# Attention output written transposed by its own products, and state space output products in four column tiles

## What is computed

```python
# memory attention (4 heads of 128, 256 keys) and latent attention (8 heads, values of 64)
s = jnp.einsum('bqhd,bkhd->bhqk', q, k) * scale        # the latent one with a mask over chunks of 64
pr = jax.nn.softmax(s, axis=-1)
o = jnp.einsum('bhqk,bkhd->bqhd', pr, v)               # then o @ w_o (1024 columns)

# state space branch: 32 groups of 64 complex states, 16 channels each
y = (jnp.einsum('blgp,gcp->blgc', h_re, c_re)
     - jnp.einsum('blgp,gcp->blgc', h_im, c_im))
y = y.reshape(b_, l_, SSM_WIDTH) + d * u
z = jax.nn.gelu(y)                                     # then z @ w_glu

merged = gates[0] * br_a + gates[1] * br_b + gates[2] * br_c
x = x + merged @ w_out
x = x + hierarchical_moe(rmsnorm(x, g_ffn))            # 32 experts, two per token
```

## Time and profile before

| | |
|---|---|
| median of 3 runs | 646.52 us (645.71 to 647.54) |
| profiled execution | 645.93 us |
| its span, first to last instruction | 644.1 us |
| granted TensorE clock, mean | 0.999 |
| TensorE busy (MATMUL rows) | 611.7 us, 95% |
| weight loads | 378.5 us, 59% |
| VectorE busy | 329.3 us, 51% |
| ScalarE busy | 170.9 us, 27% |
| GpSimd busy | 149.7 us, 23% |
| HBM | 149.9 MB read and written, 233 GB/s over the span |

### The profile page before, as it was taken

The page is one execution under the profiler, slowest core; times in us unless marked ns, Lnnn a source line. Parts: engine busy times, 40 slices in busy tenths (PEclk is TensorE's granted clock), DMA queues, the critical chain, the costliest instruction groups (busy, mean ns, idle before and its releaser), DMA issues.

```text
span 644.1 us, 9883 instructions
## 1 busy us (share of the span) xinstructions
PE 611.7 (95%) x3674; PEld 378.5 (59%) x3674; DVE 329.3 (51%) x878; ACT 170.9 (27%) x540; POOL 149.7 (23%) x341
## 2 busy tenths in 40 slices
PE   9999999999999999999999999998999999986785
PEld 6788867776556667666677767853443343332341
DVE  2434846868874588783133322675435335334233
ACT  5534234321678433221100101121221121120100
POOL 1695726733584433410000000000000000000000
PEclk9999999999999999999999999999999999999999
DMA  9783553222301523323389991098999999999993
GB/s 301 176 284 115 193 159 99 66 67 93 101 2 33 168 95 99 99 66 98 107 236 404 399 386 64 10 383 345 417 417 413 418 416 417 417 418 417 416 409 126
DMA packets 61681, 150.55 MB, mean 234 GB/s; under 512 B 12352, under 2 KB 40448, under 8 KB 53696
## 3 DMA queue, kind: packets, MB, share of 16 engines
q1 hardware_dynamic: 61632, 149.89, 62.7%
HBM read 147.12 MB, written 2.76 MB: 233 GB/s over the span
## 4 chain that ended last, share of the span: by engine, by line
PE 83%; SPq 9%; DVE 4%; DMA 2%; ACT 1%; issue 1%
PE PS L819 30%; PE PS L829 20%; SPq L704 6%; PE PS L1188 5%; PE PS L1096 5%; PE PS L1227 3%; SPq L708 3%; PE PS L1217 3%; DMA E<-in_w_e 2%; PE PS L943 2%; PE PS L966 2%; PE PS L894 2%; PE PS L883 1%; PE PS L800 1%; PE PS L1008 1%; PE PS L951 1%
## 5 line engine op out<-in xcount | busy, mean ns | idle before, releaser
L819 PE MATMUL PS<-hT,W 128*128 128x320 f32 x448 | 125.9, 436 | 0.0
L819 PEld LDWEIGHTS PS<-hT,W 128*128 128x128 f32 x448 | 83.6, 190 | 37.5 <-issue 5.2
L1188 PE MATMUL PS<-E,xT 128*32 128x256 f32 x1024 | 58.6, 379 | 9.5 <-issue 8.4
L1188 PEld LDWEIGHTS PS<-E,xT 128*32 128x32 f32 x1024 | 35.4, 110 | 36.9 <-issue 20.4
L2152 POOL TENSOR_SCALAR means<-sums 128x4 f32<-128x4 f32 (+3 forms) x35 | 7.9, 225 | 189.2 <-ACT junk L1325 188.2
L1096 PE MATMUL PS<-h,S 128*128 128x512 f32 (+1 forms) x96 | 48.2, 625 | 0.7 <-DVE S L1939 0.7
L1227 PE MATMUL PS<-yb,WG 128*128 128x512 f32 (+1 forms) x96 | 40.9, 622 | 4.0 <-DVE X L2080 3.1
L829 PE MATMUL PS<-W,hT 128*128 128x256 f32 (+5 forms) x256 | 41.7, 353 | 0.0
L2080 DVE TENSOR_TENSOR X<-X,PS 128x512 f32<-128x512 f32 (+1 forms) x48 | 32.9, 686 | 8.3 <-PE PS L1227 6.7
L829 PEld LDWEIGHTS PS<-W,hT 128*128 128x128 f32 (+1 forms) x256 | 31.5, 163 | 8.4 <-issue 1.3
L829 PE MATMUL PS<-W,mergedT 128*128 128x384 f32 (+3 forms) x192 | 35.7, 381 | 0.0
(11 more groups left out here) (313 smaller groups left out, 959.0 us busy)
## 6 DMA issues: line engine op xcount, KB each, us to landing
E<-in_w_e SPq DMA_DIRECT2D x93, 1024.0 KB, 21.8
W<-in_w_in SPq DMA_DIRECT2D x7, 1536.0 KB, 7.2
W<-in_w_in SPq DMA_DIRECT2D x7, 1024.0 KB, 6.6
W<-in_w_mem_kv SPq DMA_DIRECT2D x4, 1024.0 KB, 6.1
W<-in_w_glu SPq DMA_DIRECT2D x4, 768.0 KB, 8.0
W<-in_w_out SPq DMA_DIRECT2D x2, 1536.0 KB, 15.4
E<-in_w_e SPq DMA_DIRECT2D x6, 512.0 KB, 18.8
X<-in_x_prompt SPq DMA_DIRECT2D x4, 512.0 KB, 4.4
```

Source lines behind the costliest of these rows:

```text
L819: ins = mm(out[:, 0:TOK], w[:, k, cols:cols + 128], rhs[:, k, :], start=(k == 0), stop=(k == kt - 1))
L1188: ins = mm(PS[r:r + B, 2 + par, 0:FF], xT[:, k, place_ + B * n:place_ + B * n + B], E13[slot][:, :, k, 128 * j:128 * j + 128], start=(k == ...
```

## The change

- The step OT is gone. O makes the output feature-major at once: the values are stationary (128 columns for memory, 64 for latent), PT streams (128 or 64 columns); with values of 64, two heads go to the two column halves of the array (`across_ = 2`). ScalarE empties O straight into `oTmem` or `oTmla`.
- The division by the sums moves from the output to P: `shares(m)` on VectorE waits until the exponentials are there, takes the reciprocal and multiplies the whole of P(m) in place. It runs at VectorE's step S(m+1), ahead of that step's maximum; for the last unit at its own step PT. TensorE's PT(m) waits for it (`shares_ready`).
- `s5_y(t)` makes the products of four turns at once in four column tiles, at turns 5, 9 and 13 and at the end. There are five state buffers (`STATES`) in place of four.
- The order list changes with it: without OT, `spent` grows less, and some turns start at another step. Turn 6 came before gateC(3) and now comes behind it, directly ahead of memory's PT(4). SyncE's load of the first expert waits for the last O in place of the last OT.

```diff
+STATES = 5
@@ attention_order
-            if n - 1 == len(units) or units[n - 1][1] != units[n - 2][1]:
-                yield "OT", units[n - 2][1]
@@ emptier
-        return {"S": "act", "PT": "act", "O": "dve", "OT": "act"}[unit[1]]
+        return "act"
@@ block.tensor
-            def s5_y(q):
-
-                t = q // 4
-                pe.wait_ge(s["h_state"], q + 2)
-                if q % 4 == 0 and t > 0:
+            def s5_y(t):
+
+                pe.wait_ge(s["h_state"], 4 * t + 4)
+                if t > 0:
                     pe.wait_ge(s["y_skipped"], t)
                 for c in range(2):
-                    for n in (q, q + 1):
-                        r = 32 * (n % 4)
-                        ins = mm(PS[r:r + 32, YB, 0:TOK], wC[:, c, t, r:r + 32], hS[:, n % 4, c, :], start=(c == 0), stop=(c == 1))
+                    for n in range(4):
+                        r = 32 * n
+                        ins = mm(PS[r:r + 32, YB, 0:TOK], wC[:, c, t, r:r + 32], hS[:, (4 * t + n) % STATES, c, :], start=(c == 0), stop=(c == 1))
@@ s5_turn
-                if q % 2 == 1 and q > 1:
-                    s5_y(q - 3)
+                if q % 4 == 1 and q > 1:
+                    s5_y(q // 4 - 1)
@@ attention
                     elif step == "PT":
-                        emptied((kind, "S", m))
+                        pe.wait_ge(s["shares_ready"], unit0 + m + 1)
...
-                        dv = MD if mem_ else VH
-                        for x in range(nh):
+                        across_ = 1 if mem_ else 2
+                        for i in range(heads // across_):
                             for b, rows_ in enumerate(kb):
-                                for c in range(parts):
-                                    h = h0 + nh * c + x
+                                for r in range(across_):
+                                    c, x = divmod(across_ * i + r, nh)
+                                    h = h0 + across_ * i + r
...
-                                    ins = mm(out[n * c:n * c + n, dv * x:dv * x + dv], PT[0:rows_, m % 2, at:at + n], rhs,
+                                    w = 128 // across_
+                                    ins = mm(out[w * r:w * r + w, n * i:n * i + n], values, PT[0:rows_, m % 2, at:at + n],
@@ block.vector
+                def shares(m):
+                    _, nh = across(units[m])
+                    nk = sum(key_blocks(units[m]))
+                    w = soft[:, (unit0 + m) % 4]
+                    dve.wait_ge(*emptied_at(UNIT_NO[kind, "S", m]))
+                    link(V_.reciprocal(w[:, 2, 0:nh], w[:, 1, 0:nh]))
+                    p = P[:, m % 2, 0:nh * nk].rearrange("p (h k) -> p h k", h=nh)
+                    V_.tensor_tensor(p, p, w[:, 2, 0:nh, None].broadcast_to([128, nh, nk]), ALU.mult).then_inc(s["shares_ready"], 1)
+
+                if step == "PT" and m == len(units) - 1:
+                    shares(m)
                 if step == "S":
+                    if m > 0:
+                        shares(m - 1)
```

More of the change, by code:

```diff
@@ L225, in attention @@
     def attention(kind, units, each):
-        whole = []
         for step, m in attention_order(units):
-            if step == "OT":
-                whole.append(m)
-                continue
             if m == len(units) - 1 and step in ("PT", "O"):
@@ L235, in attention @@
                 fill(each)
-                while whole:
-                    put(kind, "OT", whole.pop(0))
-        return whole
     started = False
@@ L263, in middle @@
             fill()
-    whole = attention("mem", MEM_UNITS, 1)
+    attention("mem", MEM_UNITS, 1)
     for t in range(NT):
@@ L271, in middle @@
         put("qlT", t)
-    for t in whole:
-        put("mem", "OT", t)
     for j in range(len(KEYS)):
@@ L288, in middle @@
     held, pace, due = False, LATE_PACE, spent
-    whole = attention("mla", MLA_UNITS, 1)
+    attention("mla", MLA_UNITS, 1)
     fill(1)
-    for t in whole:
-        put("mla", "OT", t)
     while turn < GP:
@@ L486, in build @@
         (ckT, qlT, V, kT), _ = place(at8, ("ckT", [128, 2, 576]), ("qlT", [128, 3, TOK]), ("V", [128, 5, 512]), ("kT", [128, H, 576]))
-        (braw, bpad, craw, cpad), _ = place(at9, ("braw", [128, 2, GP, CH]), ("bpad", [128, 2, GP, 2, CH]), ("craw", [128, 2, 4, ST]),
+        (braw, bpad, craw, cpad), at10 = place(at9, ("braw", [128, 2, GP, CH]), ("bpad", [128, 2, GP, 2, CH]), ("craw", [128, 2, 4, ST]),
                                             ("cpad", [128, 2, 4, 2, ST]))
-        (P, PT, O), at10 = place(at9, ("P", [128, 2, 512]), ("PT", [128, 2, 512]), ("O", [128, NT, 512]))
+        (P, PT), _ = place(at9, ("P", [128, 2, 512]), ("PT", [128, 2, 512]))
         (early,), at11 = place(at10, ("early", [128, NEARLY]))
@@ L719, in _ @@
             sp.dma_start(brow[:, NG:], a["b_re"][0].rearrange("g e -> (g e)").partition_broadcast(128)).then_inc(s["router_loaded"], 16)
-            done(("mla", "OT", NT - 1))
+            done(("mla", "O", len(MLA_UNITS) - 1))
             load_up(0)
@@ L921, in attention @@
                     out = begin((kind, step, m))
[L922 to L929, removed]
+                    unit0 = 0 if mem_ else len(MEM_UNITS)
+                    _, t, h0, heads = units[m]
                     f, n = TILES[t]
@@ L1019, in branch @@
                     if d == 0:
-                        emptied(("mem" if kind == "outC" else "mla", "OT", NT - 1))
+                        emptied(("mem", "O", len(MEM_UNITS) - 1) if kind == "outC" else ("mla", "O", len(MLA_UNITS) - 1))
                     feature_major((kind, d), use(f"{kind}{g}"), col, oTmem if kind == "outC" else oTmla, 4)
@@ L1042, in _ @@
                 elif kind == "last_y":
-                    s5_y(GP - 2)
+                    s5_y(GP // 4 - 1)
             pe.wait_ge(s["z_ready"], 4)
@@ L1406, in attention @@
                 unit0, oT = (0, oTmem) if kind == "mem" else (len(MEM_UNITS), oTmla)
-                if step == "OT":
-                    f, n = TILES[m]
-                    empty(oT[:, :, f:f + n], full((kind, "OT", m))[:, 0:4 * n].rearrange("p (j n) -> p j n", j=4))
+                t, n = units[m][1], 128
+                if step == "O":
+                    f, n = TILES[t]
+                    j0, nj = (x * (MD if kind == "mem" else VH) // 128 for x in units[m][2:])
+                    empty(oT[:, j0:j0 + nj, f:f + n], full((kind, "O", m))[:, 0:nj * n].rearrange("p (j n) -> p j n", j=nj))
                     return
-                t, n = units[m][1], 128
                 _, nh = across(units[m])
@@ L1701, in turn_back @@
                 cos_, sin_ = tabs[q % 2][:, 0, :], tabs[q % 2][:, 1, :]
-                if q >= 4:
-                    dve.wait_ge(s["y_full"], q - 3)
+                if q >= STATES:
+                    dve.wait_ge(s["y_full"], q - STATES + 1)
                 st.after(scanned[q])
-                dst = hS[:, q % 4]
+                dst = hS[:, q % STATES]
                 m1 = st.mark(V_.tensor_tensor(dst[:, 0], rotB[:, 0], cos_, ALU.mult))
@@ L1726, in attention @@
             def attention(kind, units, step, m):
-                if step not in ("S", "O"):
-                    return
                 unit0 = 0 if kind == "mem" else len(MEM_UNITS)
[L1730 to L1734, removed]
-                if step == "S":
+                def shares(m):
[8 more added lines that the diff above has]
+                    shares(m)
+                if step == "S":
+                    if m > 0:
+                        shares(m - 1)
+                    t, n = units[m][1], 128
+                    _, nh = across(units[m])
+                    nk = sum(key_blocks(units[m]))
+                    w = soft[:, (unit0 + m) % 4]
                     src = full((kind, "S", m))[:, 0:nh * nk]
@@ L1745, in attention @@
                             .then_inc(s["scores_max"], 1)
[L1746 to L1755, removed]
             def turned(out, x, cos_, sin_, a_, b_):
```

8 lines of the change are left out of this document (4 added, 4 removed).

## The result

The changed kernel takes 648.79 us (median of 11 runs, 647.81 to 651.21), against 646.52 (645.57 to 647.54, 11 runs) before: ratio 1.0041, 95% interval 1.0029 to 1.0052. It is slower by 2.3 us. The forecast was 646.1, no measurable difference; 648.79 lies in its range of 641.0 to 650.4, close to the 649.4 of rival E (the clock falls in the longest pause), which had a chance of 0.07.

What follows compares the result with a forecast made beforehand. TensorE was taken to set the pace up to 418 us, with the DMA-bound expert stage passing changes through; work of -8.45 and waits of 8.0 gave -0.45, so 646.52 became 646.1 us, range 641.0 to 650.4.

Steps and rivals of the forecast that it cites:

- rival E: TensorE's clock falls in the 3.55 us pause ahead of memory's PT(4): 647.8 to 650.4, say 649.4; chance 0.07.
- s5_y: State space output products: four calls of 1.20 us in place of eight, four column tiles running at once; 4.80 us less.
- OT: Transposes of the attention output: six steps vanish from TensorE's chain; 2.68 us less.
- O, latent prompt tiles: Latent attention's output products, six units at 0.60 us each in two column tiles; 1.63 us less.
- O, memory sample tile: Memory attention's output products for the sample tile: 16 loads of 128 columns, 1.68 against 1.02; 0.66 us more.
- work alone: Sum of TensorE's work changes in state space output, output transposes and output products, without new waits: -8.45 us.
- wait of PT(0) and PT(1): Memory attention's first two transposes of P wait for VectorE to scale the shares; 2.2 us together.
- wait of PT(4): Memory's last transposes of P wait while VectorE does turn 6's six operations, then the shares; 3.55 us.
- wait of latent PT(3): Latent attention's transposes of P wait for shares because VectorE is behind from turn 11 to turn 12; 1.8 us.
- wait of gateB(5): Projection in latent attention needs the bank that S(4)'s later exponentials empty; 0.4 us.
- Rivals A and B: New attention waits: A, none real, 638.1, chance 0.09; B, only the 3.55 us one, 641.6, chance 0.18.
- C: VectorE's shares stretch to 1.28 us beside GpSimd's table building, 3.6 us more in the attention waits: 649.7; chance 0.13.

Runs made afterwards that it cites:

- run 3: Changed kernel with the state space output products in pairs of turns, two column tiles and four state buffers as before; 652.74 us, ratio 1.0090.
- run 4: Changed kernel with the scaling of all shares from the second unit on one step sooner in VectorE's queue; 640.86 us, ratio 0.9910.
- run 5: Changed kernel with turn 6 put back before gateC(3), as in the kernel before; 643.14 us, ratio 0.9944.
- run 2: Changed kernel with seven unread products on TensorE filling the wait ahead of memory's PT(4); 646.54 us, ratio 1.0001.
- run 1: Changed kernel with the shares of memory's last unit scaled one step sooner on VectorE, ahead of turn 6; 643.11 us, ratio 0.9947.

## Why the prediction failed

Compared with before, in us:

| term | predicted | measured, and where |
|---|---|---|
| s5_y | -4.80 | -4.7: 8 x 1.20 less 4 x 1.22; 4.6 by run 3 |
| OT | -2.68 | gone |
| O, latent prompt tiles | -1.63 | -1.7 on the chain: 5 x 0.25 and 1.03 - 0.59 |
| O, memory sample tile | +0.66 | +0.71: 1.73 - 1.02 |
| work alone | -8.45 | -7.6 by run 4, -7.1 by run 5; -7.5 to -8.0 in the profiles |
| wait of PT(0) and PT(1) | 2.2 | 2.03 |
| wait of PT(4) | 3.55 | 3.54 |
| wait of latent PT(3) | 1.8 | 1.35 |
| wait of gateB(5) | 0.4 | 0.17 |
| waits | 8.0 | 7.1 |
| clock | 0 | +2.5 by run 2, 2.4 by run 1; 1.7 in the profiled execution |
| sum | -0.45 | +1.9 to +2.5, against +2.27 of the medians |

In the profiled executions the span is 1.9 longer: 0.5 ahead of 90 us, then -7.6 + 7.1 + 1.7 up to the expert stage, and 0.2 in it.

- **Bound and stage.** Right. The expert stage, from the piece at 418.10 before and at 419.75 after to the end of the span, is 226.0 and 226.2 long.
- **The waits.** Right in number, place and nearly in size: walking VectorE's and TensorE's orders side by side gave 3.55 for a wait that is 3.54. The late next one, latent PT(3), and gateB(5) behind it were there too. Rivals A and B are out, and so is C: no wait is over its forecast, and the shares take 0.69 in the median (0.84 at most), not 1.28.
- **The work.** 0.9 to 1.3 too much by the medians of runs 4 and 5, which are uncertain by about as much; 0.4 to 1.0 by the profiles. There the stretch from the second 128x384 projection to the start of the expert stage, less waits, fall and added products, is 7.5 to 8.0 us shorter than the 327.94 of before in the changed kernel and in runs 1, 2, 4 and 5. In run 4's profile, which has no fall there, the steps taken from each start to the next start, less the waits, add up so: s5_y -4.75, OT -2.73, O of the latent prompt tiles -2.1, O of memory +0.7, the transposes of P +0.5, the scores +0.2, the rest +0.1: -8.0. So the terms that the prediction priced were not too large. It put the steps around them at nothing, and the transposes and scores last longer; that they now follow other steps is the likely reason. The miss nearly cancels against the waits, which came out 0.9 under their forecast.
- **The step that failed** is the last one, rival E's condition: "In the profile a pause of 3.0 us, 436 to 439, keeps the granted clock at 1.00, the 2.4 GHz level; this one is longer." From one row at 3.0 a fall at 3.55 was given a chance of 0.07. It came, and this alone moves the result from no difference to slower: with the pause kept and TensorE busy in it the time was 646.54 (run 2). The price that E named, 1.7 to at most 4.3, holds the 2.5 measured; 1.7, its lower end, is what the profiled execution lost.
- **Why the row misled.** It covers the pause and nothing behind it, and in the changed kernel the column reads 1.00 in the pause as well (144 to 146). That the profiled execution of before did keep its clock is seen from its mean of 0.999 and from the 1.92 us of the products behind the pause. But it is one execution. The same pause, ahead of the transposes of the experts' first hidden rows, stands in all twelve profiles of this study at 3.02 or 3.03 us, and the clock fell right behind it in ten of them; it was kept in that of before and in the one with six multiplications. First before, then the changed kernel, where the same products take 3.61:

```profile
439.02 0.33 PE L1197 MATMUL PS<-cst,hid 128*128 128x128 f32 x1 [3.03 <-DVE hid L2049]
```

```profile
440.65 0.33 PE L1180 MATMUL PS<-cst,hid 128*128 128x128 f32 x1 [3.02 <-DVE hid L2034]
...
441.46 3.61 PE L1200 MATMUL PS<-E,hidT 128*32 128x512 f32 x16
```

  The ten include the run with four multiplications, the kernel before with a pause of 0.91 added. The mean clock of 55 other executions of the kernel before itself, 0.989 to 0.996 (medians 0.992 and 0.993), says the same: run 2's profile reads 0.994 with the clock under 1.00 at two places of the expert stage and in the last half microsecond alone. So the eights at those places in the profile of after are no effect of the change. They also cost next to nothing: the expert stage is 226.2 with them and 226.0 without. A fall is paid for where TensorE sets the pace, as it does up to 418 us. It would have been fair to see that a row of 3.0 at 1.00 says little of 3.55.

## What to carry to other kernels

Scaling before the transpose in place of at the eviction moves a VectorE operation onto TensorE's path; put it at the first place in the queue where its input is there (run 4: one step sooner turns +2.3 us into -5.9), and look at what the order list moves directly ahead of it (run 5). Price a pause of TensorE by its length. Where TensorE sets the pace, add the clock: here nothing clear of the noise at 0.9 and 1.8 us, 1.5 to 1.7 in each profiled execution at 2.75 to 3.7, and 2.1 to 2.5 in the medians at 3.5 and 3.7. Where the pause can't be removed, products that nobody reads keep the clock up and gave 2.5 us back (run 2). One profiled execution that keeps its clock in a pause is not evidence that the next one will: look behind the pause, not in it, and compare the mean clocks of several executions.

## What the hardware showed unexpectedly

- Length alone doesn't decide. Pauses of 2.75 and 2.76 us lowered the clock in both kernels' profiled executions, while pauses of 3.03 and 3.05 (at 596.72) kept it in that of before. In the profile with four multiplications it fell behind one of 1.69:

```profile
594.10 3.39 PE L1219 MATMUL PS<-E,hidT 128*32 128x512 f32 x16 [1.69 <-issue]
...
594.00:596.00 2.00, 1.91 (x12) 0.73 (x16) 0.00 (x0) 0.00 (x0) 0.00 (x0) 0.60 1.02 426
```

  The Trainium skill (TensorE: Matmul & The Clock Gate, The HAM clock gate) says that the activity window is free-running and isn't reset when a kernel starts; that the same pause had both outcomes agrees with that, and no run here shows the window itself.
- Where the low clock falls differs: in the changed kernel mostly on gateC(4) (5.91), with ten multiplications on PT(4), O(3) and part of the projection (1.09, 1.92 and 4.79, in the kernel before 0.60, 1.06 and 4.47). The sum is about the same: 1.7 and 1.6 us from PT(4) to O(4).
- A product of P by a constant (tensor_scalar), 128 x 512, takes VectorE 0.45, that by the shares (tensor_tensor) 0.69.
